# A three-product fp32 kernel whose weight halves are multiplied in a new order: the low half last, in a run of its own

## The chip, the core and the metric

The kernel runs on one core of a Trainium2 chip. The core has a matrix engine (PE, with its weight loads shown apart as PEld), a vector engine (DVE), a scalar engine (ACT), a general engine (POOL) and a queue that issues transfers (SP). The metric is the time of one execution on the device in microseconds (us). A change counts here as faster or slower when the time differs by more than 0.2%.

## The reference

One layer of a hybrid decoder on 512 tokens of width 2048, all in fp32:

```
a = rmsnorm(h);  z = a @ w_in            # 33 tiles of 128 columns
  -> S5 state-space group, pooling group, gated linear attention (4 heads)
h = h + concat(s5, pool, gla) @ w_out    # 16 tiles
f = conv_glu_ffn(rmsnorm(h), w_up, conv_w, conv_b, w_down)   # d_ff 5632
h = h + f
h = h + (p @ w_ple) * sigmoid(rmsnorm(h) @ w_pg)             # 16 tiles
return rmsnorm(h)
```

## The kernel before

Everything is kept with features on the 128 partitions and the 512 tokens along the free axis. A weight tile is 128 output columns by all of k, cut into k-pieces of 128. To keep fp32 accuracy from the fast fp32r products, each operand is split in two: `hi` is the operand rounded to fp32r, `lo` is what is left. One k-piece is then three matmuls that add up in one PSUM bank: `w_hi*x_hi` (L629 in the trace), `w_hi*x_lo` (L630) and `w_lo*x_hi` (L631). The helper `product` issues the three, `tile` repeats them over k. So the weight half `w_lo` is needed by the third matmul of a tile.

The halves are made on the fly. A transfer brings the raw tile (1 MB; 704 KB in the down projection) to `w_raw`, ACT rounds it to `w_hi` (L1001; L1256 for the blocks of the fast stage) and signals `hi_made` or `blk_hi`, DVE subtracts it to get `w_lo` (L1401, L1763) and signals `lo_made` or `blk_lo`. There are two slots for tiles, so the halves of tile n+2 are made when the products of tile n are done (`tile_done`). PE waits for `lo_made` (`blk_lo`) ahead of the first matmul of every tile or block.

The stages in order of time: 33 tiles with W_in (n = 0 to 32, 16 k-pieces each), 16 tiles with W_out (`OUT0` on), 6 standard tiles of W_up (`STD0` on), then 41 pairs of W_up columns by a Strassen-like scheme (`fast_pair`): 7 block products of 8 k-pieces and 256 tokens each, 287 blocks, in a ring of four block slots. Then 64 tiles with W_down (`DOWN0` on; four quarters of 16 tiles, 11 k-pieces each), the small products with W_ple, and 16 tiles with W_pg.

Work of the mixers stands inside the tiles of the W_in stage, written out by hand: the callback `before(k)` of a tile issues it ahead of k-piece k. At k = 8 of tiles 27 and 29 PE issues a product of the pooling group (L743) and then `head_norm` (L665), which sums the squares of a head. DVE and ACT make the inverse root of it and spread it on a diagonal (`rms_small`, ending with L1456, semaphore `o_diag`). At k = 15 of the same tile PE waits for `o_diag` and issues the matmul L672. Tile 31 has the same two hooks without the pooling product; in tile 32 the second one is at k = 12. Tile 25 has at k = 8 the last quarter of a gate product, `glu(3)` (L731), which waits for a sigmoid of ACT (L1125). In the first quarter of the down projection, `before(k)` of the even tiles waits for the low half of the activations of k-piece k (`mid_lo_made`, DVE L1882), which are made while the first tile runs.

On DVE all is in order of writing; before the norm of tile 27 it does the states of the head before (`head_state`, L1569 and L1571, started by PE's L795 at the end of tile 26), the gate of the next head (`head_gate`), the low half of tile 28 (L1401) and the scaling of that head (`head_scale`).

Of the kernel before, what the change touches and what calls it, by code (L numbers as in the profile page):

```python
# [21 lines left out]
P = 128  # L22
SEQ = 512
D = 2048
KT = D // P
# [3 lines left out]
QT = FT // QUARTERS  # L29
# [16 lines left out]
N_U, N_Q, N_K, N_G, N_V, N_POOL, N_R = 0, 4, 8, 12, 13, 21, 25  # L46
# [87 lines left out]
def build(nc, A):  # L134
    with ExitStack() as ctx:
# [278 lines left out]
        def num(i, each, at):  # L414

            return at if i is None else each * i + at
# [36 lines left out]
        def in_bank(n):  # L453

            return n if n < 4 else n % 2
# [170 lines left out]
        def _(pe):  # L626
# [6 lines left out]
            def rank_tile(slot, out):  # L633
# [4 lines left out]
                    last = nc.tensor.matmul(out, w, xs_lo[:, k, :], start=False, stop=k == KT - 1)  # L638
                last.then_inc(tile_done, 1)

            def tile(slot, out, x_h, x_l, kts, before=None, front=False):


                for k in range(kts):
                    if before is not None:
                        before(k)
                    ks = slice(k * P, (k + 1) * P)
                    last = product(out, w_hi[slot][:, ks], w_lo[slot][:, ks], x_h[:, k, :], x_l[:, k, :],
                                   k == 0, k == kts - 1)
# [173 lines left out]


            for n in range(IN_TILES):
                pe.wait_ge(*((lo_begun, n + 1) if n < 2 else (lo_made, n + 1)))
                if n >= 4:
                    pe.wait_ge(evacuated, n - 1)

                def before(k, n=n):  # L830
                    if n < 2 and k == KT // 2:
                        pe.wait_ge(lo_made, n + 1)
                    if n == 0:
                        pe.wait_ge(xs_lo_made, k + 1)
# [12 lines left out]
                    if n in norm_slot and k == (KT - 4 if n == IN_TILES - 1 else KT - 1):  # L847
                        h = norm_slot.index(n)
                        spread(o_diag, h + 1, QKV[:, h, :], bank[2], o_spread)

                if n == N_G:
                    rank_tile(n % 2, bank[in_bank(n)][0:2 * RANK, :])
                else:
                    tile(n % 2, bank[in_bank(n)][:], xs_hi, xs_lo, KT, before, front=n == IN_TILES - 1)
                for c in range(S5_BATCHES):
                    if n == TURN_SLOT + 2 * c:
                        turn_push(c)
                    if n == READ_SLOT + 2 * c:
                        read_states(c)
                for c in range(S5_BATCHES):  # L860
                    if n == DRIVE_SLOT + 2 * c:
                        spread_intra(c)
                        drive_states(c)
                s = n - HEAD_SLOT
                if s >= 3 and s % 2 == 1:
                    head_o((s - 3) // 2)
                if s in (0, 2, 4, 6):
                    head_logits(s // 2)
                if s == 1:
                    glu(0)  # L870
                    glu(1)
                if s in (1, 3, 5, 7):
                    head_turn((s - 1) // 2)
                if s in (2, 4, 6, 8):
                    head_kv((s - 2) // 2)
                if s == 2:
                    glu(2)
                if s in (4, 6):
                    mix_pool(s - 4)


            for n in (OUT0, OUT0 + 1):
                pe.wait_ge(lo_made, n + 1)
                pe.wait_ge(evacuated, n - 1)

                def before(k, n=n):
                    if n == OUT0:
                        pe.wait_ge(xs_lo_made, KT + k + 1)

                tile(n % 2, bank[n % 2][:], xs_hi, xs_lo, KT, before)  # L890
            with pe.Fori(1, KT // 2) as i:
                for s in range(2):
                    pe.wait_ge(lo_made, 2 * i + (OUT0 + s + 1))
                    pe.wait_ge(evacuated, 2 * i + (OUT0 + s - 1))
                    tile((OUT0 + s) % 2, bank[(OUT0 + s) % 2][:], xs_hi, xs_lo, KT, front=s == 1)


            for i in range(STD_PAIRS):
                for s in range(2):
                    n = STD0 + 2 * i + s  # L900
                    pe.wait_ge(lo_made, n + 1)
                    pe.wait_ge(evacuated, n - 1)

                    def before(k, n=n):
                        if n == STD0:
                            pe.wait_ge(xs_lo_made, 2 * KT + k + 1)
                            if k == 8:
                                sum_tokens(2 * KT, [ss], bank[2], sum_spread)
                            if k == KT - 2:
                                spread(diag_made, 2, val[:], bank[2], rstd_spread)  # L910

                    tile(n % 2, bank[n % 2][:], xs_hi, xs_lo, KT, before)

            def fast_pair(i, c, first=False):

                for b in range(PRODUCTS):
                    pe.wait_ge(blk_lo, num(i, FAST_UNROLL * PRODUCTS, PRODUCTS * c + b + 1))
                    if first:
                        pe.wait_ge(xb_lo_made, MADE_BEFORE[b])
                    if b == 0 and c >= 2:  # L920
                        pe.wait_ge(c12_made, num(i, FAST_UNROLL, c - 1))
                        pe.wait_ge(c11_made, num(i, FAST_UNROLL, c - 1))
                    if b == 0 and c == 1 and i is not None:
                        pe.wait_ge(evacuated, DOWN0)
                    if b == A12:
                        pe.wait_ge(m1_kept, num(i, FAST_UNROLL, c + 1))
                    if b == A22:
                        pe.wait_ge(u3_made, num(i, FAST_UNROLL, c + 1))
                    if b == S4:
                        pe.wait_ge(c22_made, num(i, FAST_UNROLL, c + 1))  # L930
                    fresh = b in (S3, S2, A11, S1)
                    out, w_h, w_l = place(c, b), ring(w_hi, c, b), ring(w_lo, c, b)
                    for k in range(HALF_K):
                        ks = slice(k * P, (k + 1) * P)
                        last = product(out, w_h[:, ks], w_l[:, ks], xb[b][0][:, k, :], xb[b][1][:, k, :],
                                       fresh and k == 0, k == HALF_K - 1, not fresh)
                    last.then_inc(product_done, 1)

            fast_pair(None, 0, True)
# [6 lines left out]
            def down_tiles(q):  # L946
                hi, lo = mids[q % 2]
                with pe.Fori(0, KT // 2) as i:
                    for s in range(2):
                        n = KT * q + 2 * i + (DOWN0 + s)  # L950
                        pe.wait_ge(lo_made, n + 1)
                        pe.wait_ge(evacuated, n - 1)

                        def before(k, s=s):
                            if s == 0 and (q == 0 or k == 0):
                                pe.wait_ge(mid_lo_made, k + 1 if q == 0 else QT * (q + 1))

                        tile((DOWN0 + s) % 2, bank[(DOWN0 + s) % 2][:], hi, lo, QT, before)

            for q in range(QUARTERS):  # L960
                down_tiles(q)
# [15 lines left out]
            spread_sum(3 * KT, ss[:], bank[2])  # L977
            with pe.Fori(0, KT // 2) as i:
                for s in range(2):
                    pe.wait_ge(lo_made, 2 * i + (PG0 + s + 1))  # L980
                    pe.wait_ge(evacuated, 2 * i + (PG0 - 2 + s - 1))
                    before = (lambda k: pe.wait_ge(xs_lo_made, 3 * KT + k + 1)) if s == 0 else None
                    tile((PG0 + s) % 2, bank[(PG0 + s) % 2][:], xs_hi, xs_lo, KT, before)
            pe.wait_ge(squared, 4 * KT)
            sum_tokens(4 * KT - 1, [ss, sq], bank[2], sum_spread)
            spread(diag_made, 3, val[:], bank[2], rstd_spread)
# [1273 lines left out]
```

## Time and profile before

| | us |
|---|---|
| median of 3 runs (2288.44 to 2290.18) | 2289.96 |
| the profiled execution | 2287.76 |
| its span, first to last instruction | 2286.1 |
| PE busy | 2221.2 (97%) |
| PEld busy | 1963.6 (86%) |
| DVE busy | 1413.0 (62%) |
| ACT busy | 836.6 (37%) |

The span is what the trace covers. The mean granted clock of PE was 0.989 of its full 2.4 GHz. Matmuls are pipelined: the length of one in the trace holds its drain too, so two that follow without a gap start about 0.23 us apart at 512 columns, although each is shown with 0.39 us.

### The profile page before, as it was taken

The numbers are of one execution on the slowest core, as the hardware profiler recorded it, in microseconds if no ns is written. First come the engines' busy times: TensorE is split into PE (matmuls) and PEld (weight loads), VectorE is DVE, ScalarE is ACT, GpSimd is POOL, SyncE is SP. The second block draws the span as 40 slices with busy tenths as digits, with TensorE's granted clock in tenths as the row PEclk, the third lists the DMA queues.
The fourth block names the chain that finished last, engine by engine and source line by source line (L and its number), as shares of the span: only waits on it lengthen the run. The fifth ranks groups of instructions, "written<-read, shape, count | busy, mean of one in ns | idle before, by whom it ended". The sixth has DMA issues, their size and how long they took to land.

```text
span 2286.1 us, 32868 instructions
## 1 busy us (share of the span) xinstructions
PE 2221.2 (97%) x13216; PEld 1963.6 (86%) x13216; DVE 1413.0 (62%) x1570; ACT 836.6 (37%) x948; POOL 332.9 (15%) x294
## 2 busy tenths in 40 slices
PE   8999999999998999999999999998999999999995
PEld 6787878888877999999999999997888888888884
DVE  7586235553368988888888888885333333346444
ACT  6222245442243444444444444443222222226441
POOL 5992004000000111111111111110000000000001
PEclk9999999999999999999999999999999999999997
DMA  5322322133422333333322333344333332233221
GB/s 217 123 72 92 106 84 79 56 111 126 154 106 81 120 115 118 124 124 124 124 106 106 119 124 124 124 162 173 115 116 124 118 122 89 101 109 111 92 92 74
DMA packets 58442, 260.13 MB, mean 114 GB/s; under 512 B 6256, under 2 KB 15088, under 8 KB 37904
## 3 DMA queue, kind: packets, MB, share of 16 engines
q1 hardware_dynamic: 54864, 247.81, 30.1%
q0 software_dynamic: 3520, 11.54, 1.3%
q8 instruction: 38, 0.62, 0.1%
q14 instruction: 20, 0.16, 0.0%
HBM read 237.30 MB, written 22.02 MB: 113 GB/s over the span
## 4 chain that ended last, share of the span: by engine, by line
PE 86%; POOL 6%; DVE 4%; DMA 1%; ACT 1%; issue 1%; SPq 0%; DVEq 0%; POOLq 0%; ACTq 0%
PE bank L629 28%; PE bank L631 28%; PE bank L630 27%; DVE xs_lo L1424 1%; PE bank L731 1%; DVE xs_lo L1422 1%; DMA w_raw<-in_w_down 0%; DVE x_block_lo L1757 0%; DMA Y<-in_x 0%; PE bank L811 0%; DVE Y L1960 0%; PE bank L665 0%; DVE w_lo L1401 0%; POOL Q L2110 0%; DVE w_lo L1763 0%
## 5 line engine op out<-in xcount | busy, mean ns | idle before, releaser
L629 PE MATMUL bank<-x_block_hi,w_hi 128*128 128x256 f32 x2296 | 649.7, 283 | 10.3 <-DVE w_lo L1763 8.7
L631 PE MATMUL bank<-x_block_hi,w_lo 128*128 128x256 f32 x2296 | 649.6, 283 | 0.0
L630 PE MATMUL bank<-x_block_lo,w_hi 128*128 128x256 f32 x2296 | 647.0, 282 | 0.0
L1001 ACT ACTIVATE w_hi<-w_raw 128x2048 fp32r<-128x2048 f32 (+1 forms) x132 | 218.6, 1656 | 739.2 <-PE bank L631 731.1
L629 PE MATMUL bank<-xs_hi,w_hi 128*128 128x512 f32 x1120 | 444.6, 397 | 11.7 <-DVE w_lo L1408 10.4
L629 PEld LDWEIGHTS bank<-x_block_hi,w_hi 128*128 128x128 f32 x2296 | 438.8, 191 | 11.5 <-DVE w_lo L1763 10.5
L630 PEld LDWEIGHTS bank<-x_block_lo,w_hi 128*128 128x128 f32 x2296 | 439.2, 191 | 0.0
L631 PEld LDWEIGHTS bank<-x_block_hi,w_lo 128*128 128x128 f32 x2296 | 438.6, 191 | 0.0
L630 PE MATMUL bank<-xs_lo,w_hi 128*128 128x512 f32 x1120 | 437.4, 391 | 0.0
L631 PE MATMUL bank<-xs_hi,w_lo 128*128 128x512 f32 x1120 | 437.2, 390 | 0.0
L1401 DVE TENSOR_TENSOR w_lo<-w_raw,w_hi 128x2048 fp32r<-128x2048 f32 (+1 forms) x134 | 267.3, 1994 | 109.1 <-ACT w_hi L1001 106.2
L629 PEld LDWEIGHTS bank<-xs_hi,w_hi 128*128 128x128 f32 x1120 | 211.5, 189 | 59.4 <-DVE w_lo L1408 10.4
L630 PEld LDWEIGHTS bank<-xs_lo,w_hi 128*128 128x128 f32 x1120 | 211.2, 189 | 45.6 <-issue 2.9
L631 PEld LDWEIGHTS bank<-xs_hi,w_lo 128*128 128x128 f32 x1120 | 211.1, 188 | 44.4
L1763 DVE TENSOR_TENSOR w_lo<-w_raw,w_hi 128x1024 fp32r<-128x1024 f32 x147 | 199.9, 1360 | 46.8 <-ACT w_hi L1256 46.5
L1256 ACT ACTIVATE w_hi<-w_raw 128x1024 fp32r<-128x1024 f32 x147 | 155.6, 1059 | 182.3 <-DVE w_raw L1768 61.9
L1763 DVE TENSOR_TENSOR w_lo<-Y,w_hi 128x1024 fp32r<-128x1024 f32 x140 | 191.7, 1369 | 43.9 <-ACT w_hi L1256 43.4
L1256 ACT ACTIVATE w_hi<-Y 128x1024 fp32r<-128x1024 f32 x140 | 148.3, 1059 | 169.8 <-PE bank L631 58.4
L1907 DVE TENSOR_TENSOR Y<-Y,bank 128x512 f32<-128x512 f32 x64 | 44.0, 688 | 251.7 <-PE bank L631 251.7
L629 PE MATMUL bank<-mid_a_hi,w_hi 128*128 128x512 f32 x352 | 140.0, 398 | 8.0 <-DVE w_lo L1401 8.0
L630 PE MATMUL bank<-mid_a_lo,w_hi 128*128 128x512 f32 x352 | 139.7, 397 | 0.0
L631 PE MATMUL bank<-mid_a_hi,w_lo 128*128 128x512 f32 x352 | 139.7, 397 | 0.0
(310 smaller groups left out, 2543.2 us busy)
## 6 DMA issues: line engine op xcount, KB each, us to landing
w_raw<-in_w_up SPq DMA_DIRECT2D x48, 1024.0 KB, 5.4
w_raw<-in_w_down SPq DMA_DIRECT2D x64, 704.0 KB, 4.1
Y<-in_w_up SPq DMA_DIRECT2D x40, 1024.0 KB, 6.0
w_raw<-in_w_in SPq DMA_DIRECT2D x32, 1024.0 KB, 4.9
w_raw<-in_w_out SPq DMA_DIRECT2D x16, 1024.0 KB, 4.9
w_raw<-in_w_pg SPq DMA_DIRECT2D x16, 1024.0 KB, 4.8
mid_kept<-val POOLq DMA_DIRECT2D x44, 256.0 KB, 2.3
mid_raw<-mid_kept SPq DMA_DIRECT2D x15, 512.0 KB, 5.2
```

The lines of the kernel that those rows point to most:

```text
L629: nc.tensor.matmul(out, w_h, x_h, start=first, stop=False, skip_group_check=onto)
L630: nc.tensor.matmul(out, w_h, x_l, start=False, stop=False, skip_group_check=onto)
L631: return nc.tensor.matmul(out, w_l, x_h, start=False, stop=last, skip_group_check=onto)
L731: m = nc.tensor.matmul(bank[(6, 7, 5, 5)[j]][:], Y[:, 12 + k, j * P:(j + 1) * P], Y[:, k, :], start=k == 0, stop=k == S5_TILES - 1)
L1001: nc.scalar.activation(w_hi[c % 2][:, 0:width], w_raw[c % 2][:, 0:width], ACT.Copy).then_inc(hi_made, 1)
L1256: nc.scalar.activation(ring(w_hi, c, b), raw_block(c, b), ACT.Copy).then_inc(blk_hi, 1)
L1401: tt(w_lo[c % 2][:, 0:width], w_raw[c % 2][:, 0:width], w_hi[c % 2][:, 0:width].bitcast(F32), ALU.subtract).then_inc(lo_made, 1)
L1422: ins = tt(xs_lo[:, k, :], Y[:, k, :], hi, ALU.subtract)
L1424: ins = stt(xs_lo[:, k, :], Y[:, k, :], par(gain, k), hi, ALU.mult, ALU.subtract)
L1763: tt(ring(w_lo, c, b), raw_block(c, b), ring(w_hi, c, b).bitcast(F32), ALU.subtract).then_inc(blk_lo, 1)
L1907: tt(Y[:, j, :], Y[:, j, :], bank[n % 2][:], ALU.add).then_inc(evacuated, 1)
```

## The change

A new helper `tile_low_last` issues, for all k, only the two products with `w_hi`, then waits for `w_lo`, then issues the products with `w_lo` for all k. The wait ahead of the tile is now for `hi_made` alone. It is used for W_in tiles 2 to 31 but 13, for W_out tile `OUT0 + 1` and the even ones after it, for five of the six standard tiles, for all 64 down tiles and for the odd tiles of W_pg. The blocks of `fast_pair` are reordered in the same way with `blk_hi` and `blk_lo`. Tile 32, `OUT0`, `STD0`, the odd W_out tiles, the even W_pg tiles and the small products keep the old order. What is computed, the number of matmuls and all code of the other engines stay.

```diff
+            def tile_low_last(slot, out, x_h, x_l, kts, low, before=None):
+                for k in range(kts):
+                    if before is not None:
+                        before(k)
+                    w = w_hi[slot][:, k * P:(k + 1) * P]
+                    nc.tensor.matmul(out, w, x_h[:, k, :], start=k == 0, stop=False)
+                    nc.tensor.matmul(out, w, x_l[:, k, :], start=False, stop=False)
+                pe.wait_ge(lo_made, low)
+                for k in range(kts):
+                    last = nc.tensor.matmul(out, w_lo[slot][:, k * P:(k + 1) * P], x_h[:, k, :], start=False,
+                                            stop=k == kts - 1)
+                last.then_inc(tile_done, 1)
...
             for n in range(IN_TILES):
-                pe.wait_ge(*((lo_begun, n + 1) if n < 2 else (lo_made, n + 1)))
+                late = n >= 2 and n != N_G and n < IN_TILES - 1
+                pe.wait_ge(*((lo_begun, n + 1) if n < 2 else (hi_made if late else lo_made, n + 1)))
...
+                elif late:
+                    tile_low_last(n % 2, bank[in_bank(n)][:], xs_hi, xs_lo, KT, n + 1, before)
...
             for n in (OUT0, OUT0 + 1):
-                pe.wait_ge(lo_made, n + 1)
+                pe.wait_ge(hi_made if n > OUT0 else lo_made, n + 1)
...
                 for b in range(PRODUCTS):
-                    pe.wait_ge(blk_lo, num(i, FAST_UNROLL * PRODUCTS, PRODUCTS * c + b + 1))
+                    pe.wait_ge(blk_hi, num(i, FAST_UNROLL * PRODUCTS, PRODUCTS * c + b + 1))
...
                     for k in range(HALF_K):
-                        ks = slice(k * P, (k + 1) * P)
-                        last = product(out, w_h[:, ks], w_l[:, ks], xb[b][0][:, k, :], xb[b][1][:, k, :],
-                                       fresh and k == 0, k == HALF_K - 1, not fresh)
+                        for part in range(2):
+                            nc.tensor.matmul(out, w_h[:, k * P:(k + 1) * P], xb[b][part][:, k, :],
+                                             start=fresh and k == 0 and part == 0, stop=False,
+                                             skip_group_check=not fresh)
+                    pe.wait_ge(blk_lo, num(i, FAST_UNROLL * PRODUCTS, PRODUCTS * c + b + 1))
+                    for k in range(HALF_K):
+                        last = nc.tensor.matmul(out, w_l[:, k * P:(k + 1) * P], xb[b][0][:, k, :], start=False,
+                                                stop=k == HALF_K - 1, skip_group_check=not fresh)
...
                         n = KT * q + 2 * i + (DOWN0 + s)
-                        pe.wait_ge(lo_made, n + 1)
+                        pe.wait_ge(hi_made, n + 1)
...
-                        tile((DOWN0 + s) % 2, bank[(DOWN0 + s) % 2][:], hi, lo, QT, before)
+                        tile_low_last((DOWN0 + s) % 2, bank[(DOWN0 + s) % 2][:], hi, lo, QT, n + 1, before)
```

The first place is PE at the end of W_in tile 27, before; L672 is the matmul that needs `o_diag`, L806 the first one behind the tile:

```order
L630 MATMUL bank<-xs_lo,w_hi 128x512
L631 MATMUL bank<-xs_hi,w_lo 128x512
L629 MATMUL bank<-xs_hi,w_hi 128x512
L630 MATMUL bank<-xs_lo,w_hi 128x512
L631 MATMUL bank<-xs_hi,w_lo 128x512
L672 MATMUL bank<-QKV,ones 128x512 [waits o_diag]
L629 MATMUL bank<-xs_hi,w_hi 128x512
L630 MATMUL bank<-xs_lo,w_hi 128x512
L631 MATMUL bank<-xs_hi,w_lo 128x512
L806 MATMUL bank<-sc,v_tok 128x128 [waits logits_out,S_made,sc_masked]
```

Now (L647 and L648 are the two products with `w_hi`, L651 the one with `w_lo`, L686 is the old L672, L820 the old L806):

```order
L647 MATMUL bank<-xs_hi,w_hi 128x512
L648 MATMUL bank<-xs_lo,w_hi 128x512
L686 MATMUL bank<-QKV,ones 128x512 [waits o_diag]
L647 MATMUL bank<-xs_hi,w_hi 128x512
L648 MATMUL bank<-xs_lo,w_hi 128x512
L651 MATMUL bank<-xs_hi,w_lo 128x512 [waits lo_made]
L651 MATMUL bank<-xs_hi,w_lo 128x512 x15
L820 MATMUL bank<-sc,v_tok 128x128 [waits logits_out,S_made,sc_masked]
```

Between the last row of `head_norm` and this wait stood 7 k-pieces of three matmuls, and now 7 of two; the third ones moved behind it.

The second place is PE in the first of the down tiles, before, at its first k-pieces:

```order
L629 MATMUL bank<-mid_a_hi,w_hi 128x512 [waits mid_lo_made,evacuated]
L630 MATMUL bank<-mid_a_lo,w_hi 128x512
L631 MATMUL bank<-mid_a_hi,w_lo 128x512
L629 MATMUL bank<-mid_a_hi,w_hi 128x512 [waits mid_lo_made]
L630 MATMUL bank<-mid_a_lo,w_hi 128x512
L631 MATMUL bank<-mid_a_hi,w_lo 128x512
```

Now, at its last two k-pieces with `w_hi` and the run behind them:

```order
L647 MATMUL bank<-mid_a_hi,w_hi 128x512 [waits mid_lo_made]
L648 MATMUL bank<-mid_a_lo,w_hi 128x512
L647 MATMUL bank<-mid_a_hi,w_hi 128x512 [waits mid_lo_made]
L648 MATMUL bank<-mid_a_lo,w_hi 128x512
L651 MATMUL bank<-mid_a_hi,w_lo 128x512 [waits lo_made]
L651 MATMUL bank<-mid_a_hi,w_lo 128x512 x10
```

The waits for the activations' low half were three matmuls apart and are two apart now, and the wait for `w_lo` moved from the head of the tile to behind 22 matmuls.

## Rows read from the trace of the kernel before

**Rows 1.** Waits of PE over the span: waiter, releaser, us in total, times, longest.
```profile
PE bank L629 <- DVE w_lo L1763: 8.7, 3, 3.7
PE bank L629 <- DVE w_lo L1401: 8.6, 3, 6.2
PE bank L681 <- POOL QKV L2084: 6.6, 4, 3.3
```
**Rows 2.** PE groups by form: operation, count, busy us, mean ns, idle before, releasers.
```profile
L629 PE MATMUL bank<-x_block_hi,w_hi 128*128 128x256 f32 x2296 | 649.7, 283 | 10.3 <-DVE w_lo L1763 8.7 <-DVE u_two L1786 0.8 <-DVE val L1793 0.8
L630 PE MATMUL bank<-x_block_lo,w_hi 128*128 128x256 f32 x2296 | 647.0, 282 | 0.0
```
**Rows 3.** Timeline of PE, end of tile 27: start us, us, instruction, idle before.
```profile
387.90 0.39 PE L631 MATMUL bank<-xs_hi,w_lo 128*128 128x512 f32 x1
388.13 1.02 PE L672 MATMUL bank<-QKV,ones 128*128 128x512 f32 x2
```
**Rows 4.** Timeline of DVE during tile 27.
```profile
374.39 0.42 DVE L1569 COPY S<-bank 128x256 f32<-128x256 f32 x1 [2.28 <-PE bank L795]
...
381.42 2.28 DVE L1401 TENSOR_TENSOR w_lo<-w_raw,w_hi 128x2048 fp32r<-128x2048 f32 x1
...
385.55 0.15 DVE L1451 TENSOR_SCALAR norm<-bank 128x4 f32<-128x4 f32 x1
...
386.98 0.69 DVE L1456 TENSOR_TENSOR QKV<-ident,norm 128x512 f32<-128x512 f32 x1
```
**Rows 5.** Timeline of PE, the same hook in tiles 29 and 31.
```profile
424.60 0.59 PE L672 MATMUL bank<-QKV,ones 128*128 128x512 f32 x1
...
458.35 0.59 PE L672 MATMUL bank<-QKV,ones 128*128 128x512 f32 x1
```
**Rows 6.** Timeline of DVE, the norms of tiles 29 and 31.
```profile
423.45 0.69 DVE L1456 TENSOR_TENSOR QKV<-ident,norm 128x512 f32<-128x512 f32 x1
...
453.66 0.16 DVE L1451 TENSOR_SCALAR norm<-bank 128x4 f32<-128x4 f32 x1 [1.67 <-PE bank L665]
...
455.11 0.69 DVE L1456 TENSOR_TENSOR QKV<-ident,norm 128x512 f32<-128x512 f32 x1
```
**Rows 7.** Timelines of ACT and PE around the hook of tile 25.
```profile
341.78 0.69 ACT L1125 ACTIVATE Y<-bank,params_sb 128x512 f32<-128x512 f32 x1
...
344.32 1.88 PE L731 MATMUL bank<-Y 128*128 128x512 f32 x4
```
**Rows 8.** Timelines of ACT and PE at the second W_out tile.
```profile
482.51 1.90 ACT L1001 ACTIVATE w_hi<-w_raw 128x2048 fp32r<-128x2048 f32 x1
...
491.31 0.50 PE L629 MATMUL bank<-xs_hi,w_hi 128*128 128x512 f32 x1 [0.64 <-DVE w_lo L1401]
```
**Rows 9.** Timelines of PE and DVE, blocks 5 and 6 of the first fast pair.
```profile
755.75 0.42 DVE L1786 TENSOR_TENSOR u_two<-u_two,bank 128x256 f32<-128x256 f32 x1
...
756.31 0.36 PE L629 MATMUL bank<-x_block_hi,w_hi 128*128 128x256 f32 x1 [0.84 <-DVE u_two L1786]
...
759.61 0.41 DVE L1793 TENSOR_TENSOR val<-u_two,bank 128x256 f32<-128x256 f32 x1
```
**Rows 10.** Timelines of PE, DVE and ACT at the first three down tiles.
```profile
1565.22 0.48 PE L629 MATMUL bank<-mid_a_hi,w_hi 128*128 128x512 f32 x1 [1.77 <-DVE w_lo L1401]
...
1569.17 1.88 DVE L1882 TENSOR_TENSOR mid_a_lo<-Y,mid_a_hi 128x512 fp32r<-128x512 f32 x3
...
1583.79 1.38 ACT L1001 ACTIVATE w_hi<-w_raw 128x1408 fp32r<-128x1408 f32 x1 [2.74 <-DMA w_raw<-in_w_down]
...
1587.07 0.77 PE L629 MATMUL bank<-mid_a_hi,w_hi 128*128 128x512 f32 x1 [6.20 <-DVE w_lo L1401]
```
**Rows 11.** Windows: stretch, us, busy (count) of PE, PEld, DVE, ACT, POOL, clock, DMA.
```profile
109.80:113.00 3.20, 3.01 (x11) 2.76 (x12) 3.13 (x5) 1.00 (x2) 3.08 (x6) 0.50 0.00 0
...
1565.30:1568.70 3.40, 3.40 (x15) 2.76 (x16) 3.40 (x6) 1.61 (x4) 0.00 (x0) 1.00 0.31 131
...
1587.00:1591.00 4.00, 3.94 (x9) 3.14 (x10) 3.16 (x4) 0.47 (x1) 0.00 (x0) 0.50 0.69 201
```

More of the change, by code:

```diff
@@ L888, in before @@
                         pe.wait_ge(xs_lo_made, KT + k + 1)
-                tile(n % 2, bank[n % 2][:], xs_hi, xs_lo, KT, before)
+                if n > OUT0:
+                    tile_low_last(n % 2, bank[n % 2][:], xs_hi, xs_lo, KT, n + 1, before)
+                else:
+                    tile(n % 2, bank[n % 2][:], xs_hi, xs_lo, KT, before)
             with pe.Fori(1, KT // 2) as i:
                 for s in range(2):
-                    pe.wait_ge(lo_made, 2 * i + (OUT0 + s + 1))
+                    pe.wait_ge(lo_made if s else hi_made, 2 * i + (OUT0 + s + 1))
                     pe.wait_ge(evacuated, 2 * i + (OUT0 + s - 1))
-                    tile((OUT0 + s) % 2, bank[(OUT0 + s) % 2][:], xs_hi, xs_lo, KT, front=s == 1)
+                    if s:
+                        tile((OUT0 + s) % 2, bank[(OUT0 + s) % 2][:], xs_hi, xs_lo, KT, front=True)
+                    else:
+                        tile_low_last(OUT0 % 2, bank[OUT0 % 2][:], xs_hi, xs_lo, KT, 2 * i + (OUT0 + 1))
             for i in range(STD_PAIRS):
@@ L900, in _ @@
                     n = STD0 + 2 * i + s
-                    pe.wait_ge(lo_made, n + 1)
+                    pe.wait_ge(hi_made if n > STD0 else lo_made, n + 1)
                     pe.wait_ge(evacuated, n - 1)
@@ L910, in before @@
                                 spread(diag_made, 2, val[:], bank[2], rstd_spread)
-                    tile(n % 2, bank[n % 2][:], xs_hi, xs_lo, KT, before)
+                    if n > STD0:
+                        tile_low_last(n % 2, bank[n % 2][:], xs_hi, xs_lo, KT, n + 1, before)
+                    else:
+                        tile(n % 2, bank[n % 2][:], xs_hi, xs_lo, KT, before)
             def fast_pair(i, c, first=False):
                 for b in range(PRODUCTS):
-                    pe.wait_ge(blk_lo, num(i, FAST_UNROLL * PRODUCTS, PRODUCTS * c + b + 1))
+                    pe.wait_ge(blk_hi, num(i, FAST_UNROLL * PRODUCTS, PRODUCTS * c + b + 1))
                     if first:
@@ L979, in _ @@
                 for s in range(2):
-                    pe.wait_ge(lo_made, 2 * i + (PG0 + s + 1))
+                    pe.wait_ge(hi_made if s else lo_made, 2 * i + (PG0 + s + 1))
                     pe.wait_ge(evacuated, 2 * i + (PG0 - 2 + s - 1))
-                    before = (lambda k: pe.wait_ge(xs_lo_made, 3 * KT + k + 1)) if s == 0 else None
-                    tile((PG0 + s) % 2, bank[(PG0 + s) % 2][:], xs_hi, xs_lo, KT, before)
+                    if s:
+                        tile_low_last((PG0 + s) % 2, bank[(PG0 + s) % 2][:], xs_hi, xs_lo, KT, 2 * i + (PG0 + s + 1))
+                    else:
+                        tile(PG0 % 2, bank[PG0 % 2][:], xs_hi, xs_lo, KT,
+                             lambda k: pe.wait_ge(xs_lo_made, 3 * KT + k + 1))
             pe.wait_ge(squared, 4 * KT)
```

1 line of the change is left out of this document (removed).

## The prediction

> **What bounds the kernel now.** I read the busy shares first: PE is busy for 97% of the span, the next engine for 62%, so only PE's own gaps can be won. Next the waits of PE [rows 1]: the reader is to see how few are for a low half. Three are for blocks of the fast stage (8.7 us) and three for whole tiles (8.6 us). That is 17.3 us that the change can touch, in six places of some 450 tiles and blocks. Elsewhere the low half has long been there, and a wait that is already met is free: of the 2296 first products in the fast stage, 287 stand behind a wait, and all their idle time, 10.3 us, has a named releaser in five places; their mean, 283 ns, is that of the second products without any wait, 282 ns [rows 2]. So the steady state neither gains nor loses. What counts is what stands at the six places, and what the new order moves elsewhere.
>
> **Part 1: hooks inside a tile come earlier.** This the change does without meaning to. The callback `before(k)` of a tile stood behind 3k matmuls and now stands behind 2k. PE issues one every 0.23 us [rows 3], so a hook at k = 15 is reached 15 x 0.23 = 3.4 us sooner and one at k = 8 is reached 1.8 us sooner, while the tile as a whole still takes 48 matmuls. A wait that was met by a small margin becomes a stall, and the products with `w_lo` that could fill it stand behind it in the queue.
> Tile 27: PE comes to L672 at 388.13 and goes on at once [rows 3]. The diagonal it needs ends at 386.98 + 0.69 = 387.67 [rows 4], a margin of 0.46. In the new order PE is there at 384.7. Does the diagonal come earlier too, since `head_norm` does? No: DVE starts at 374.39, released by the end of tile 26, and its norm at 385.55 follows with no idle time noted, behind the states, the gate, the low half at 381.42 and the scaling [rows 4]. It is DVE's own queue that sets 387.67. PE stalls 387.7 - 384.7 = 3.0 us.
> Tile 29 repeats it: reached at 424.60 [rows 5], ready at 424.14 [rows 6], so reached at 421.2 now and stalled 2.95 us.
> Tile 31: reached at 458.35 [rows 5], so 454.9 now. Here DVE had 1.67 us idle before its norm at 453.66 [rows 6] and can start with the earlier sums, at about 452.0; the diagonal takes 2.14 from there (453.66 to 455.80), so it is ready at 454.15. No stall. Tiles 0, 1 and 32 keep the old order.
> Tile 25: the gate product was reached at 344.32 and is reached at 342.5 now; its sigmoid ends at 342.47 [rows 7]. That is 0 to 0.1 us, taken as 0. Hooks of tiles 2 and 3 also come earlier; PE then waits for POOL (four waits, 6.6 us [rows 1]), which would swallow the some tenths of a us.
> Sum of part 1: **+6.0 us**; nothing behind gives it back, since no wait of PE on DVE's low halves stands between these tiles and W_out that could swallow it [rows 1]. Bounds: 0, if DVE's queue should turn out to follow the sums after all, and +6.4.
>
> **Part 2: the clock after these stalls.** After the 3.3 us wait for POOL the granted clock is 0.50, that is 1.2 GHz, for a stretch of 3.2 us [rows 1, 11]; after the 1.77 us wait at 1565 it stays 1.00, 2.4 GHz [rows 10, 11]. A low stretch of 3.2 us costs 1.6. A stall of 3.0 lies nearer to the first: I take 1.0 for each of the two, bounds 0 and 1.6. **+2.0 us** (0 to 3.2).
> The Trainium skill, "TensorE: Matmul & The Clock Gate", section "HAM oscillation — how this bites in real kernels", says that a burst that follows a long enough gap starts at the low clock and pays each time. By that rule it is the full price both times and the sum would be 1.2 higher; the trace agrees on its 3.3 us gap.
>
> **Part 3: the second W_out tile.** Its 0.64 us wait for the low half goes: its high half was made at 484.4, long before 491.31, and the low half, made just before 491.31, is needed only behind 32 matmuls, 7 us into the tile [rows 8]. With the slower restart (0.50 instead of 0.39), **-0.7 us**; bounds -0.8 and 0.
>
> **Part 4: start of the fast stage.** The three waits there, 8.7 us [rows 1], shrink, by up to the 16 high products of a block at an estimated 0.12 us (half of 0.23), 1.9 us each. Yet the end does not move: block 5 waits for `u3_made`, ready at 755.75 + 0.42 = 756.17, and block 6 for `c22_made`, ready at 760.02, both on DVE [rows 9]. DVE splits the activations' blocks there, and neither of the two rows notes a wait of DVE for PE. What PE gains before is idle time at 756. What is late next is this DVE chain, and all of the gain is lost in it. One cost is left: block 4 ends earlier, so the gap ahead of block 5 grows from 0.84 us to several, and the clock may be low in it. Its 24 products take 2.9 us at full rate and 1.6 more in a low stretch, so it ends at 760.8 and not before 760.17; 0.6 at two chances in three. **+0.4 us**, bounds 0 and +1.3.
>
> **Part 5: the first three down tiles.** The first started at 1565.22 after 1.77 us [rows 10]; its high half is ready, so it starts at about 1563.4. But its waits for the activations' low halves are now two matmuls apart. The last three of these end at 1569.17 + 1.88 = 1571.05 [rows 10]; then come one pair (0.46) and the run of 11 low products (2.5), so the tile ends at 1574.1. Before it ended at 1565.22 + 33 x 0.23 = 1572.8: the gain of 1.8 turns into a loss of 1.3. The second tile ends at 1581.7. The third waited 6.20 us and started at 1587.07. Its high half waits for a transfer and is made at 1583.79 + 1.38 = 1585.17 [rows 10], so PE starts at 1585.2: 1.85 us sooner, and the loss of the first tile is swallowed by this idle time. The clock was 0.50 from 1587 to 1591, where 9 matmuls ran instead of 17 [rows 11], a loss of 1.85; with 3.5 us idle instead of 6.2 I take a loss of 1.1. Together **-2.5 us**, bounds -3.7 and -1.8.
>
> **The rest.** All other tiles and blocks keep their times: as many matmuls and weight loads, as many semaphore signals from the same last matmul, one more wait each, already met. DVE, ACT, POOL and SP run the same code; their next work is released by `tile_done` as before. No wait moves past a transfer.
>
> **Sum.** +6.0 + 2.0 - 0.7 + 0.4 - 2.5 = +5.2 us on the profiled execution, 2287.76 to 2293.0. The median of the runs is 2.2 above that execution, so the forecast is **2295.2 us**. Own range of this case: low ends of the parts 2 to 5 give +6.0 + 0 - 0.8 + 0 - 3.7 = +1.5, high ends +6.4 + 3.2 + 0 + 1.3 - 1.8 = +9.1, so 2291.5 to 2299.1, most of it below 2298.
>
> **Rivals.**
> *The stalls of part 1 do not come.* DVE's or ACT's work in tiles 27 and 29 shifts with the earlier sums, by its own slack. For it: the sums do come 1.8 us sooner, and in tile 31 DVE did wait for them [rows 6]. Against: no idle time is noted in DVE's rows of tile 27 [rows 4]. Then -0.7 + 0.4 - 2.5 = -2.8, 2287.2 us, not slower. It decides as soon as the diagonal is ready 2.5 us sooner.
> *The rate of matmuls changes.* Pairs with one weight and runs with one kind of moving operand replace triples. The trace has no such run. Some 12,500 matmuls are reordered, so 0.25 ns each way is 3 us; the mean of the second kind is 1 ns under that of the first [rows 2], and if such a nanosecond is lost on half of them it is 6 us. By this 2289 to 2301, either sign; 2301 as its slow end.
> *A wait in the middle of a stream costs.* 401 waits for a low half now stand between matmuls that ran on without a break. The weight load of the next matmul is drawn ahead of the running one; if it can't pass the wait, a part of it, 0.05 to 0.1 us, is exposed each time: +20 to +40, about 2325 us. Against it: blocks started behind waits before, and show nothing [rows 2].
> The Trainium skill, "TensorE: Matmul & The Clock Gate", section "Step-by-step: what each phase is for", says that weight loads are pulled ahead of matmuls in flight, which is what this rival would break. The trace does not show it broken at a block's start.
> *It does nothing at all*, since parts cancel: inside the first case's range, no case of its own.
>
> **How the numbers follow.** First case 0.68, no stalls 0.16, rate 0.12, waits cost 0.04. A measurement of this kernel can tell some 0.2%, 4.6 us, from no change, so slower begins at 2294.5. The forecast lies only 0.7 above it: of the first case 0.4 is slower and 0.28 within. No stalls: 0.14 within, 0.02 faster. Rate: 0.06 slower, 0.04 within, 0.02 faster. Waits: 0.04 slower. That is 0.04 faster, 0.46 same, 0.50 slower. The range takes in the first case, most of the second's and of the third's: 2287.0 to 2300.0.
>
> **What would show it.** PE idle of about 3 us before L686 (the old L672) in tiles 27 and 29, released by DVE's diagonal (old L1456), none in tile 31; a low clock behind one or both. No wait at the second W_out tile. PE waits in the first fast pair for `u_two` and `val` where it waited for low halves, with block 6 starting at the same distance from the stage's start. In the first down tile, waits for `mid_a_lo` and an end 1.3 us later; the third down tile released by ACT's `w_hi`, not DVE's `w_lo`. The spacing of matmuls unchanged. I am wrong if the norm of tiles 27 and 29 starts earlier on DVE, or if the time from the fast stage's sixth pair to its end is not the same within 1 us.

## The result, and the profile after

The changed kernel takes 2294.41 us (median of 10 runs, 2292.06 to 2296.71); the kernel before, in the same comparison, takes 2288.39 (10 runs, 2286.51 to 2290.51). The ratio is 1.0026, with a 95% interval of 1.0018 to 1.0035: slower by 6.0 us or 0.26%, beyond the 0.2% that counts here, though the lower end of the interval is not. The forecast was +5.2 us, 2295.2. The forecast time is 0.8 too high although the change was forecast 0.8 too small, since its base, the median of three runs (2289.96), stood 1.6 above that of the ten. The profiled execution took 2294.11 us with a span of 2292.4.

The page's busy times after the change; PE's is 0.9 us above that of before:

```profile
PE 2222.1 (97%) x13216; PEld 1961.3 (86%) x13216; DVE 1412.6 (62%) x1570; ACT 836.4 (36%) x948; POOL 337.4 (15%) x294
```

The waits of PE, in the columns of [rows 1]. In this kernel L647, L648 and L651 are the products of a low-last tile, L961 and L966 the high and low ones of a block, L686 is the old L672, L1490 the diagonal (old L1456):

```profile
PE bank L629 <- DVE w_lo L1442: 11.2, 1, 11.2
PE bank L686 <- DVE val L1490: 5.9, 2, 3.7
...
PE bank L686 <- DVE QKV L1490: 5.6, 2, 2.8
PE bank L961 <- DVE u_two L1820: 3.9, 1, 3.9
PE bank L961 <- ACT w_hi L1290: 3.8, 3, 1.5
...
PE bank L647 <- ACT w_hi L1035: 3.1, 1, 3.1
PE bank L961 <- ACT conv_in L1296: 2.7, 1, 2.7
PE bank L966 <- DVE w_lo L1797: 2.6, 2, 1.9
PE bank L647 <- DVE mid_a_lo L1916: 2.0, 2, 1.7
```

The reader should see both sides of the account. The first row is the start of the first W_in tile, and L686 on `val` belongs to the rms norms; the kernel before waits there too (10.4 and 5.9 us). The rows on low halves, 8.7 and 8.6 us in [rows 1], have shrunk to 2.6. In their place stand waits for `w_hi` of ACT (3.8 and 3.1), for `u_two` (3.9), `conv_in` (2.7) and `mid_a_lo` (2.0), and one row that has no counterpart before: L686 on the diagonal, twice, 5.6 us.

The reordered groups in the fast stage, in the columns of [rows 2]:

```profile
L961 PE MATMUL bank<-x_block_hi,w_hi 128*128 128x256 f32 x2296 | 561.1, 282 | 10.5 <-DVE u_two L1820 3.9 <-ACT w_hi L1290 3.8 <-ACT conv_in L1296 2.7
L961 PE MATMUL bank<-x_block_lo,w_hi 128*128 128x256 f32 x2296 | 560.2, 282 | 0.0
L966 PE MATMUL bank<-x_block_hi,w_lo 128*128 128x256 f32 x2296 | 320.9, 282 | 2.6 <-DVE w_lo L1797 2.6
```

The mean of a matmul is 282 ns as in [rows 2]. The busy sums are lower, since the instructions of one group now follow so closely that they overlap, and the overlap is counted once; they say nothing of the rate.

To see where the time went I took the start of the last matmul of each tile and block in both timelines, after minus before:

| up to the end of | shift, us | step |
|---|---|---|
| W_in tile 26 | +0.8 | first load, in the first tile |
| tile 27 | +4.0 | +3.1 |
| tile 28 | +4.0 | 0 |
| tile 29 | +8.6 | +4.7 |
| first W_out tile | +8.65 | 0 |
| second W_out tile | +7.7 | -0.9 |
| block 4 of the first fast pair | +4.6 | -3.1 |
| block 5 | +9.9 | +5.3 |
| the first fast pair | +9.05 | -0.85 |
| the second fast pair | +8.9 | -0.2 |
| last fast block | +8.9 | 0 over 273 blocks |
| first down tile | +10.1 | +1.25 |
| third down tile | +6.8 | -3.4 |
| the span | +6.3 | -0.4 |

**Tiles 27, 29 and 31.** The timeline of PE (start us, us, instruction, idle before) at the old L672 [rows 3, 5]:

```profile
388.55 1.12 PE L686 MATMUL bank<-QKV,ones 128*128 128x512 f32 x2 [2.79 <-DVE QKV L1490]
...
428.15 1.22 PE L686 MATMUL bank<-QKV,ones 128*128 128x512 f32 x1 [2.79 <-DVE QKV L1490]
...
463.63 0.59 PE L686 MATMUL bank<-QKV,ones 128*128 128x512 f32 x1
```

And DVE in tile 27, the rows that answer to [rows 4]:

```profile
375.22 0.42 DVE L1603 COPY S<-bank 128x256 f32<-128x256 f32 x1 [2.28 <-PE bank L809]
...
382.25 2.28 DVE L1435 TENSOR_TENSOR w_lo<-w_raw,w_hi 128x2048 fp32r<-128x2048 f32 x1
...
386.38 0.15 DVE L1485 TENSOR_SCALAR norm<-bank 128x4 f32<-128x4 f32 x1
...
387.81 0.69 DVE L1490 TENSOR_TENSOR QKV<-ident,norm 128x512 f32<-128x512 f32 x1
```

All of DVE's rows stand 0.83 us later than before, which is the shift that was there at tile 26. The sums came to DVE 1.8 us sooner counted from the end of tile 26, and DVE made nothing of it: its own queue sets the diagonal, and PE stands still for 2.79 us. In tile 31 PE does not wait.

**The clock.** Windows (stretch, us, busy and count of PE, PEld, DVE, ACT, POOL, clock, DMA) behind the waits of tile 27, tile 29, block 5 and the third down tile:

```profile
389.10:392.50 3.40, 3.40 (x15) 2.62 (x14) 2.16 (x3) 0.00 (x0) 0.00 (x0) 1.00 0.00 0
428.10:431.40 3.30, 3.25 (x6) 1.93 (x7) 1.13 (x2) 0.00 (x0) 0.00 (x0) 0.50 0.01 5
765.00:768.40 3.40, 3.40 (x17) 3.40 (x17) 2.68 (x3) 0.98 (x2) 0.00 (x0) 0.50 0.66 231
1595.40:1598.80 3.40, 3.40 (x10) 2.63 (x9) 3.40 (x5) 0.76 (x2) 0.00 (x0) 0.50 0.63 201
```

The two stalls have the same length. Behind the first PE keeps 2.4 GHz (1.00), behind the second it falls to 1.2 GHz (0.50); that is the 1.6 us between the steps of +3.1 and +4.7. The window of block 5 is part of a longer low stretch, which begins in the wait ahead of it:

```profile
762.60:769.30 6.70, 5.30 (x25) 5.33 (x26) 5.84 (x8) 1.33 (x2) 0.00 (x0) 0.50 0.47 174
```

**The places where a wait went.** PE at the second W_out tile (no wait now, 0.64 us in [rows 8]), at blocks 4 to 6 of the first fast pair [rows 9] and at the first and third down tile [rows 10]:

```profile
499.16 0.39 PE L647 MATMUL bank<-xs_hi,w_hi 128*128 128x512 f32 x1
...
756.96 0.35 PE L961 MATMUL bank<-x_block_hi,w_hi 128*128 128x256 f32 x1 [2.73 <-ACT conv_in L1296]
...
764.00 0.55 PE L961 MATMUL bank<-x_block_hi,w_hi 128*128 128x256 f32 x1 [3.94 <-DVE u_two L1820]
...
1574.51 0.50 PE L647 MATMUL bank<-mid_a_hi,w_hi 128*128 128x512 f32 x1 [0.31 <-DVE mid_a_lo L1916]
...
1578.79 0.50 PE L647 MATMUL bank<-mid_a_hi,w_hi 128*128 128x512 f32 x1 [1.74 <-DVE mid_a_lo L1916]
...
1594.09 0.47 PE L647 MATMUL bank<-mid_a_hi,w_hi 128*128 128x512 f32 x1 [3.11 <-ACT w_hi L1035]
```

Block 5 starts at 764.00 - 756.31 = 7.7 us after its old start, which is the shift that PE had before the stage: what was won ahead of it has become the 3.94 us wait for the DVE chain, with a low clock behind it. The third down tile waited 6.20 us for DVE's `w_lo` [rows 10] and now 3.11 us for ACT's `w_hi`.

### The profile page after: what moved, and what is told of

It is laid out like the page before. It is cut to its first block, busy times and chain, and to the rows that moved or that the text cites. A ratio compares the mean times of both kernels' runs of the same rounds, so it can differ in the third digit from the quotient of the medians.

```text
span 2292.4 us, 32868 instructions
## 1 busy us (share of the span) xinstructions
PE 2222.1 (97%) x13216; PEld 1961.3 (86%) x13216; DVE 1412.6 (62%) x1570; ACT 836.4 (36%) x948; POOL 337.4 (15%) x294
## 4 chain that ended last, share of the span: by engine, by line
PE 85%; POOL 6%; DVE 5%; DMA 1%; ACT 1%; issue 1%; SPq 0%; DVEq 0%; POOLq 0%; ACTq 0%
PE bank L961 23%; PE bank L651 13%; PE bank L647 13%; PE bank L648 13%; PE bank L966 12%; PE bank L629 3%; PE bank L631 3%; PE bank L630 3%; DVE xs_lo L1458 1%; PE bank L745 1%; DMA Y<-in_x 1%; DVE x_block_lo L1791 0%; DMA w_raw<-in_w_down 0%; PE bank L825 0%; DVE Y L1994 0%
## 5 line engine op out<-in xcount | busy, mean ns | idle before, releaser
L961 PE MATMUL bank<-x_block_hi,w_hi 128*128 128x256 f32 x2296 | 561.1, 282 | 10.5 <-DVE u_two L1820 3.9
L961 PE MATMUL bank<-x_block_lo,w_hi 128*128 128x256 f32 x2296 | 560.2, 282 | 0.0
L961 PEld LDWEIGHTS bank<-x_block_hi,w_hi 128*128 128x128 f32 x2296 | 437.8, 191 | 11.5 <-ACT w_hi L1290 7.3
L961 PEld LDWEIGHTS bank<-x_block_lo,w_hi 128*128 128x128 f32 x2296 | 437.8, 191 | 0.0
L966 PE MATMUL bank<-x_block_hi,w_lo 128*128 128x256 f32 x2296 | 320.9, 282 | 2.6 <-DVE w_lo L1797 2.6
L647 PE MATMUL bank<-xs_hi,w_hi 128*128 128x512 f32 x800 | 317.6, 397 | 0.0
L648 PE MATMUL bank<-xs_lo,w_hi 128*128 128x512 f32 x800 | 312.2, 390 | 0.0
L966 PEld LDWEIGHTS bank<-x_block_hi,w_lo 128*128 128x128 f32 x2296 | 294.7, 191 | 3.0 <-DVE w_lo L1797 3.0
L651 PE MATMUL bank<-xs_hi,w_lo 128*128 128x512 f32 x800 | 189.9, 390 | 0.0
L647 PEld LDWEIGHTS bank<-xs_hi,w_hi 128*128 128x128 f32 x800 | 151.0, 189 | 34.0 <-issue 3.3
L648 PEld LDWEIGHTS bank<-xs_lo,w_hi 128*128 128x128 f32 x800 | 150.7, 188 | 32.8 <-issue 2.2
L651 PEld LDWEIGHTS bank<-xs_hi,w_lo 128*128 128x128 f32 x800 | 150.5, 188 | 31.4
L647 PE MATMUL bank<-mid_a_hi,w_hi 128*128 128x512 f32 x352 | 140.8, 400 | 5.2 <-ACT w_hi L1035 3.1
L648 PE MATMUL bank<-mid_a_lo,w_hi 128*128 128x512 f32 x352 | 139.9, 398 | 0.0
```

Source lines behind the costliest of these rows:

```text
L647: nc.tensor.matmul(out, w, x_h[:, k, :], start=k == 0, stop=False)
L648: nc.tensor.matmul(out, w, x_l[:, k, :], start=False, stop=False)
L651: last = nc.tensor.matmul(out, w_lo[slot][:, k * P:(k + 1) * P], x_h[:, k, :], start=False, stop=k == kts - 1)
L961: nc.tensor.matmul(out, w_h[:, k * P:(k + 1) * P], xb[b][part][:, k, :], start=fresh and k == 0 and part == 0, stop=False, skip_group_chec ...
L966: last = nc.tensor.matmul(out, w_l[:, k * P:(k + 1) * P], xb[b][0][:, k, :], start=False, stop=k == HALF_K - 1, skip_group_check=not fresh)
```

## The experiments

Each was timed beside the kernel before (2288.42 us for experiments 1, 2, 4 and 5, 2288.51 for the others). "Shift" is again against the kernel before.

**1. The two tiles in the old order.**

```diff
-                late = n >= 2 and n != N_G and n < IN_TILES - 1
+                late = n >= 2 and n != N_G and n < IN_TILES - 1 and n not in (27, 29)
```

> The changed kernel, with W_in tiles 27 and 29 alone put back to the old order. Theory (hooks reached too early): both stalls of 2.8 us ahead of the matmul that needs o_diag go, and the low clock behind them, 7.8 us of the traces' shift; what is left is -0.9 at the second W_out tile, about +1 at the start of the fast stage and about -3 at the third down tile: 2 to 4 us faster than the kernel before. Rivals (another rate of matmuls, or a price for each of the 401 waits): 2 of some 400 reordered tiles and blocks change nothing, it stays 5 to 6 us slower than the kernel before.

Measured: 2284.64 us (11 runs), ratio 0.9985 (0.9976 to 0.9994). The steps at tiles 27 and 29 are gone and the second W_out tile keeps its -0.93. With two tiles in the old order the change is a gain of 3.8 us, under 0.2% but with an interval clear of 1; with them in the new order it is a loss of 6.0. The two tiles account for 7.8 us of this difference. A part of the rest is where the low clock fell: in this trace it fell on block 4 of the first fast pair and on the first down tile, ahead of the waits for DVE and for the transfer, which swallowed it:

```profile
748.50:755.20 6.70, 5.46 (x24) 5.20 (x24) 6.67 (x4) 2.58 (x4) 1.15 (x1) 0.50 0.00 0
1571.10:1574.40 3.30, 3.30 (x9) 2.53 (x9) 2.41 (x5) 0.63 (x1) 0.00 (x0) 0.50 0.80 253
```

**2. Only these two tiles.** The kernel before, with `tile_low_last` for n = 27 and 29 alone:

```diff
+                late = n in (27, 29)
+                pe.wait_ge(*((lo_begun, n + 1) if n < 2 else (hi_made if late else lo_made, n + 1)))
...
+                elif late:
+                    tile_low_last(n % 2, bank[in_bank(n)][:], xs_hi, xs_lo, KT, n + 1, before)
```

> The kernel before, with W_in tiles 27 and 29 alone in the new order. Theory: +6 us by two stalls of about 2.8 to 3.0 us, and 0 to 3.2 us by the clock, 6 to 9 us slower than the kernel before, more than the whole change. Rivals (rate, price of a wait): 0 to 0.1 us.

Measured: 2295.76 us (5 runs, 2295.11 to 2300.10), ratio 1.0043 (1.0030 to 1.0057). Its timeline of PE (here the diagonal is L1473):

```profile
388.11 1.13 PE L686 MATMUL bank<-QKV,ones 128*128 128x512 f32 x2 [2.81 <-DVE QKV L1473]
...
427.72 1.67 PE L686 MATMUL bank<-QKV,ones 128*128 128x512 f32 x2 [2.82 <-DVE QKV L1473]
```

Its windows behind the two waits, clock in the column ahead of the DMA share:

```profile
389.00:392.40 3.40, 3.40 (x16) 2.73 (x15) 2.16 (x3) 0.00 (x0) 0.00 (x0) 1.00 0.00 0
428.50:431.50 3.00, 3.00 (x8) 2.00 (x7) 2.04 (x3) 0.00 (x0) 0.00 (x0) 0.50 0.00 0
```

The shift goes from +0.4 to +3.5 to +8.25: the same two steps, with the same two clocks, and 2 of 49 W_in and W_out tiles are enough for all of the loss. The five runs fall in two groups, 2295.1 to 2295.8 and 2299.9 to 2300.1; the trace is of the first.

**3. Was it the order of the products, or where the hook stands?** The changed kernel with the same tiles low-last, but in tiles 27 and 29 the matmul that needs the diagonal is issued inside the run of low products, behind 45 matmuls of the tile as before:

```diff
                 for k in range(kts):
+                    if inside is not None:
+                        inside(k)
                     last = nc.tensor.matmul(out, w_lo[slot][:, k * P:(k + 1) * P], x_h[:, k, :], start=False,
...
-                    if n in norm_slot and k == (KT - 4 if n == IN_TILES - 1 else KT - 1):
+                    if n in norm_slot and n not in (27, 29) and k == (KT - 4 if n == IN_TILES - 1 else KT - 1):
...
+                def inside(k, n=n):
+                    if n in (27, 29) and k == 13:
+                        h = norm_slot.index(n)
+                        spread(o_diag, h + 1, QKV[:, h, :], bank[2], o_spread)
```

> The changed kernel, all in the new order, but in W_in tiles 27 and 29 the matmul that waits for o_diag is issued inside the run of low products, behind 45 matmuls of the tile as in the kernel before and not behind 30. Theory (place of the hook, not the order of the products): no stall there, 2284.6 us as when the two tiles were put back, 3 to 4.5 us faster than the kernel before. Rival (the new order in these tiles itself delays DVE's norm or PE): it stays 5 to 6 us slower than before.

Measured: 2285.95 us (11 runs), ratio 0.9986 (0.9977 to 0.9995). PE in tile 27 (L653 is the low product, L688 the old L672), with no idle time:

```profile
388.72 1.07 PE L653 MATMUL bank<-xs_hi,w_lo 128*128 128x512 f32 x4
389.63 1.02 PE L688 MATMUL bank<-QKV,ones 128*128 128x512 f32 x2
```

The shift is 1.49, 1.50, 1.54 at the ends of tiles 26, 27 and 29. The new order of the products costs nothing there; the place of the hook in PE's queue does. The gain over the kernel before, 2.6 us, is less than the 3 to 4.5 expected. Its trace, of the slowest of these runs, shows where some of it may lie: the low clock fell behind the waits at block 5 and at the third down tile, as in the changed kernel, and not ahead of them as in the trace of experiment 1.

**4. The fast stage alone.** The kernel before with the blocks of `fast_pair` as in the changed one (its edit is the part of the change's diff with `blk_hi`).

> The kernel before, with the 287 blocks of the fast stage alone in the new order. Theory: block 5 of the first pair starts at the same distance from the end of the last standard tile as before, within 0.3 us; only the clock behind the longer gap costs, 0 to 2 us in all; the later 280 blocks keep their pace to 0.1 ns a matmul. Rival rate: 280 blocks of 24 matmuls change by a few us, spread evenly. Rival price of a wait: 280 times 0.05 to 0.1 us, 14 us or more.

Measured: 2288.62 us (11 runs), ratio 1.0001 (0.9992 to 1.0010). Block 5 of the first pair in the timeline of PE:

```profile
756.40 0.55 PE L935 MATMUL bank<-x_block_hi,w_hi 128*128 128x256 f32 x1 [3.95 <-DVE u_two L1791]
```

The window behind it, at 0.50:

```profile
756.50:760.00 3.50, 3.50 (x17) 3.50 (x18) 3.47 (x4) 0.18 (x1) 0.00 (x0) 0.50 0.46 133
```

Before, this block started at 756.31 [rows 9]. Of the 8.7 us of waits for low halves 2.7 are left, and the block starts at the same time. From the end of the second pair to the end of the stage, 273 blocks, the shift stays at +1.32: 273 waits between running matmuls and some 6500 reordered matmuls cost less than can be seen. Over 273 blocks 0.1 us would be 0.4 ns for each wait, where the rival had 50 to 100.

**5. The down projection alone.** The kernel before with the 64 down tiles low-last.

> The kernel before, with the 64 down tiles alone in the new order. Theory: 2.5 to 3.5 us faster, all of it by the end of the third down tile: first tile starts 1.8 us sooner and ends 1.3 us later, third tile starts on w_hi, 1.9 us sooner than it did on w_lo, and the rest is clock. Rival (price of a wait): 64 more waits make it slower again by 3 to 6 us; rival (rate): a drift over the 61 later tiles.

Measured: 2285.25 us (11 runs), ratio 0.9988 (0.9979 to 0.9997). Counted from the end of the fast stage, the first down tile ends 2.8 us later than before (1.25 in the changed kernel; here a low stretch falls into it), the third 3.6 earlier. The low stretch begins 1.7 us after the end of a wait of 1.74 for `mid_a_lo`:

```profile
1573.70:1577.00 3.30, 3.30 (x10) 2.55 (x9) 2.44 (x4) 0.63 (x1) 0.05 (x1) 0.50 0.90 303
```

The third tile's start in the timeline of PE:

```profile
1587.36 0.47 PE L647 MATMUL bank<-mid_a_hi,w_hi 128*128 128x512 f32 x1 [1.61 <-ACT w_hi L1015]
```

The window around it, at 1.00 throughout:

```profile
1585.00:1589.00 4.00, 2.39 (x11) 1.66 (x10) 1.85 (x2) 3.25 (x4) 0.00 (x0) 1.00 0.79 316
```

**6. As 5, with the first down tile in the old order.** If that tile's loss reached the end, this kernel would be faster than 5. The edit against kernel 5, without the lines that take the first two tiles out of the loop:

```diff
-                        pe.wait_ge(hi_made, n + 1)
+                    pe.wait_ge(lo_made if first else hi_made, n + 1)
...
-                        tile_low_last((DOWN0 + s) % 2, bank[(DOWN0 + s) % 2][:], hi, lo, QT, n + 1, before)
+                    if first:
+                        tile((DOWN0 + s) % 2, bank[(DOWN0 + s) % 2][:], hi, lo, QT, before)
+                    else:
+                        tile_low_last((DOWN0 + s) % 2, bank[(DOWN0 + s) % 2][:], hi, lo, QT, n + 1, before)
```

> The kernel before, with the down tiles in the new order but the first one in the old order. Theory (what the first tile loses is swallowed by the third tile's wait for its transfer): the third tile starts at the same distance from the end of the fast stage as with all 64 in the new order, so 2285.3 us, or up to 1.6 us more by a low clock behind the longer gap. Rival (the first tile's loss reaches the end): 1.2 us faster than with all 64, 2284.0.

Measured: 2287.45 us (11 runs), ratio 0.9995 (0.9986 to 1.0005): 2.2 slower than 5, where at most 1.6 was expected. No run of 6 is as fast as any of 5 (2286.44 to 2290.47, 2283.84 to 2286.13). The third down tile in the timeline of PE:

```profile
1587.23 0.77 PE L647 MATMUL bank<-mid_a_hi,w_hi 128*128 128x512 f32 x1 [4.63 <-ACT w_hi L1024]
```

The window behind it:

```profile
1587.30:1590.70 3.40, 3.40 (x8) 2.71 (x9) 3.40 (x4) 2.00 (x3) 0.00 (x0) 0.50 0.47 123
```

The tile starts at the same time, since its transfer sets it. What the first tile no longer loses becomes idle time, 4.63 us instead of 1.61, and behind the longer gap PE runs at 1.2 GHz. Of those 3.0 us some 1.4 are the order of the products, and 1.5 the low stretch that in the trace of 5 fell into the first tile. A loss ahead of a wait was worth having here; that the longer gap is what brought the low clock is read from one trace of each kernel, and not tested apart.

**7. The wait behind it all, taken away.** The third down tile waits for its transfer in both orders. On the queue SP that transfer stood behind a wait for the last `mid_a_lo`, a 2 MB load and two loads of activations; it was issued at 1572.45. This is the kernel before, products in the old order, with SP's order changed (the cut has the main lines):

```diff
-            sp.wait_ge(mid_lo_made, QT)
-            sp.dma_start(Y[:, HALF_K:KT, :], h_dram[:, HALF_K:KT, :]).then_inc(h_in[2], 16)
...
+            mid_in_raw(0)
+            for j in (2, 3):
+                weights(DOWN0 + j, 0, A["w_down"][j], W_DOWN)
+            sp.wait_ge(mid_lo_made, QT)
+            sp.dma_start(Y[:, HALF_K:KT, :], h_dram[:, HALF_K:KT, :]).then_inc(h_in[2], 16)
...
-                        if j >= 2:
+                        if j >= 4:
```

> The kernel before in the old order of products; only SP's order changes: the activations' first chunk and the raw weights of the third and fourth down tile are issued ahead of the wait for mid_lo_made and the 2 MB transfer of h behind it. Theory (the third tile's 6.2 us wait is this queue's, not the low half's): the wait goes with the low clock behind it, 6 to 8 us faster, 2280.5 to 2282.5. Rival (HBM or the making of the halves sets it): 0 to 2 us.

Measured: 2279.33 us (5 runs), ratio 0.9958 (0.9944 to 0.9972): 9.2 us faster, more than the 6 to 8 expected (8.3 in the traces). The transfer is issued at 1565.37. The first matmul of the third down tile (L632; 1587.07 with 6.20 idle in [rows 10]) follows the last of the second:

```profile
1580.83 0.39 PE L634 MATMUL bank<-mid_a_hi,w_lo 128*128 128x512 f32 x1
1581.06 0.40 PE L632 MATMUL bank<-mid_a_hi,w_hi 128*128 128x512 f32 x1
```

The shift goes from +0.4 to -7.9 there: the 6.2 of idle time, the 1.85 of low clock of [rows 10, 11] and a slower restart. The remaining wait for a transfer was the larger prize. Which of the things ahead of the transfer counted most, the wait or the loads, was not separated.

**8. Both together.** SP's order of 7, low-last in W_in but for tiles 27 and 29, in W_out, the standard tiles, W_pg and the down tiles but the first, and the fast stage in the old order.

> SP's order of the run beside it, with the new order of products in the W_in tiles but 27 and 29, in the W_out, standard, W_pg and down tiles, and the old order in 27, 29, the fast stage and the first down tile. Theory: 0.8 us more than SP's order alone gives (the second W_out tile), 2280 to 2281.5. Rival (the new order costs by itself): slower than SP's order alone.

Measured: 2278.44 us (5 runs, 2277.51 to 2279.09), ratio 0.9956 (0.9942 to 0.9970). It beats both kernels, by 10.1 us the one before. Of that 0.9 is beyond kernel 7, which the intervals don't tell apart; the trace has it at the second W_out tile (-0.93). Once the transfer is early, what this kernel has of the new order is worth that one place.

## Why the prediction was right, step by step

**Part 1, hooks come earlier: +6.0, measured +6.2** (3.1 at tile 27, and 4.7 less the 1.6 of part 2 at tile 29). Each stall is 2.79 us of idle time and some 0.3 of restart. The hook of tile 25, taken as 0, shows as 0.1. The chain of the argument holds link by link: the diagonal is set by DVE's queue, tile 31 does not wait, and experiments 1, 2 and 3 take the loss away, bring it back alone, and tie it to the hook's place. The rival without stalls is out.

**Part 2, the clock: +2.0 (0 to 3.2), measured +1.6**, but not as two half prices: one stall cost nothing and the other the full 1.6. The Trainium skill, "TensorE: Matmul & The Clock Gate", section "HAM oscillation — how this bites in real kernels", has a burst behind a long enough gap start at the low clock each time. The trace agrees for tile 29 and not for tile 27, with the same 2.79 us; if 2.79 us is long enough for that rule, the step at tile 27 would have been 4.7 and not 3.1. The half price was not the nearest reading of the rows either. It set a stall of 3.0 us between waits of 3.3 and 1.77 [rows 1, 10], but the kernel before has two nearer ones, both in the first fast pair, and behind both the clock is low:

```profile
740.97 0.49 PE L629 MATMUL bank<-x_block_hi,w_hi 128*128 128x256 f32 x1 [2.54 <-DVE w_lo L1763]
750.84 0.39 PE L629 MATMUL bank<-x_block_hi,w_hi 128*128 128x256 f32 x1 [2.38 <-DVE w_lo L1763]
...
741.10:744.50 3.40, 3.40 (x17) 3.40 (x18) 2.28 (x2) 2.22 (x2) 0.00 (x0) 0.50 0.90 366
751.40:754.70 3.30, 3.30 (x18) 3.30 (x17) 3.30 (x3) 2.00 (x2) 0.00 (x0) 0.50 0.00 0
```

By these the full price of 3.2 was the one to take; that the sum of two half prices came nearer is luck.

**Part 3, the second W_out tile: -0.7, measured -0.9** (-0.93 in experiments 1 and 3 as well), a little beyond its bound of -0.8.

**Part 4, start of the fast stage: +0.4 (0 to 1.3), measured +1.2.** The mechanism was right: the gain is lost in DVE's chain, and block 5 starts when it did. The low clock came in full behind block 5's start, in the changed kernel and in experiments 3 and 4. Its size was too low: the stretch is 6.8 us and not 3.2, with 5.3 of it behind the start of block 5, and the measured price is near the upper bound. In experiment 1, with the same code there, the low stretch began one wait earlier, in the 2.74 us ahead of block 4, and was over before block 5 started. Block 5's wait for DVE, 1.58 us there, swallowed what it had cost, the block ran at 1.00, and the shift over the stage's start was about 0. So the place of the low stretch against the next wait that DVE sets decides whether it costs anything.

**Part 5, the first three down tiles: -2.5 (-3.7 to -1.8), measured -2.1.** The first tile's loss was put at 1.3 and is 1.25; the third starts 1.85 us sooner, as worked out, after a wait of 3.11 us where 3.5 was forecast. What was too high is the clock given back: the low stretch still costs nearly as much as before. In experiments 1 and 5 it fell into the first tile and the wait at the third swallowed it; the third tile then ran at 1.00, and the part came to -3.6, the lower bound.

**The rest: 0, measured 0** over 273 fast blocks, the standard tiles and the down tiles from the fourth on. With experiment 4 that settles the two rivals of the rate and of the price of a wait. (The 12,500 matmuls that the first of them counts are all the products of the kernel; 11,400 are reordered.) The Trainium skill, "TensorE: Matmul & The Clock Gate", section "Step-by-step: what each phase is for", says that weight loads are drawn ahead of matmuls in flight; if a met wait between two matmuls disturbed that, it cost no time that the 273 blocks show.

Step by step: 3.1 + 4.7 - 0.9 + 1.2 - 2.1 = +6.0, as in the medians; the spans of the two traces differ by 6.3, with 0.8 of the first load and -0.4 at the very end, which are not of the change. That this agrees so well is partly luck. The traces of the changed kernel and of experiment 1 share the code of the fast stage and of the down tiles, and still stand 1.2 and 1.5 us apart in them, by where the low clock fell. The forecast too gained by errors that cancel: parts 1, 2 and 3 together were forecast 0.4 too high, parts 4 and 5 together 1.2 too low. What stays open is why one stall of 2.79 us lowers the clock and the next does not. In experiment 2 three runs stand at 2295.1 to 2295.8 and two at 2299.9 and 2300.1. A low clock behind the stall of tile 27 too would explain 1.6 of these 4.5 us; no trace was taken of them, and the rest stays open.

## What to carry to other kernels

In an in-order queue an instruction's place is counted in instructions, not in loop steps: when a tile is split into two passes, everything hooked to its first pass comes earlier, and a wait with a margin of half a microsecond turns into a stall if what it waits for does not come earlier too. List every wait that sits inside the reordered loop with its margin, and move the tight ones to where they stood. Before taking work out of the way of one wait, look for the one behind it: the wait at the third down tile was worth 2 to 4 us to the new order, and 8 to a few lines on the queue that issues the transfers.

## What the runs showed of the hardware

- Equal stalls, unequal clocks: 2.79 us left the granted clock at 1.00 in tile 27 and took it to 0.50 in tile 29; 2.81 and 2.82 did the same in experiment 2. The wait of 2.7 us ahead of block 4 left it at 1.00 in the changed kernel and was followed by 0.50 in experiment 1; the wait of 1.74 us in the first down tile left it at 1.00 in the changed kernel and was followed by 0.50 in experiments 1 and 5. So the length of the last wait alone does not tell. Waits of 1.58, 1.61 and 1.77 us left it at 1.00, and 3.11, 3.94, 3.95, 4.63 and 6.20 us were followed by 0.50.
- A low stretch costs only where PE, and not the next wait, sets the time: 6.8 us at 0.50 cost 1.2 us net in the changed kernel, where block 5 started in it, and about nothing in experiment 1, where it was over before that block started.
- A wait already met, between two running matmuls, costs nothing that 273 of them in a row show (under 0.4 ns each).
- Two products with one weight, and then a run with the other, go at the rate of triples: no drift over some 6500 matmuls of 256 columns.
- Saving time ahead of a transfer that sets the next start can make a kernel slower: 6 is 2.2 us slower than 5, and in their traces the longer gap (4.63 instead of 1.61 us) is followed by the low clock.
